# Seam halves: splitting two layer ends by tokens and moving norm factors to the products in a three-layer block on one core

## The chip, the cores and the metric

One NeuronCore of a Trainium2 chip runs the whole program. The metric is the device time of one execution in microseconds. Engines: TensorE (PE) for matmuls, VectorE (DVE) and ScalarE (ACT) for elementwise work, GpSimd (POOL), which here mostly issues a few stores, and SyncE (SP), which issues the loads.

## The reference, cut to what matters

A sequence of 256 tokens with 2048 features passes two "hybrid" layers and one block of another kind. All is float32.

```python
def hybrid_layer(x, mem, w_in, ..., w_out, ln_g, ln_b):      # twice
    h = x @ w_in                                             # 2048 x 6672
    y = concat([y_a * silu(a_z), y_b * silu(b_z), y_m * silu(m_z)])   # three kinds of attention
    return layer_norm(DEEPNORM_ALPHA * x + y @ w_out, ln_g, ln_b)

def rms_norm(x, w):
    return x * rsqrt(mean(x * x) + RMS_EPS) * w

def second_block(x, ...):
    h = rms_norm(x, norm_mix_pre)
    a_q, a_f, a_i, a_g, b_q, b_k, b_v, b_f, g_a, g_b = split(h @ w_in)   # 2048 x 11272
    y_a = hgrn2_mixer(a_q, a_f, a_i, a_g, ...) @ w_up_a
    y_b = fox_mixer(b_q, b_k, b_v, b_f) @ w_up_b
    merged = sigmoid(g_a) * y_a + sigmoid(g_b) * y_b
    x = x + rms_norm(merged @ w_o, norm_mix_post)
    h = rms_norm(x, norm_ffn_pre)
    gate, up = split(h @ w_ffn_in)                           # 2048 x 11264
    return x + rms_norm((silu(gate) * up) @ w_ffn_down, norm_ffn_post)
```

## The kernel before, in words

Every float32 product is made of three fp32r products of high and low parts (high times high, high times low, low times high). An activation matrix is held feature-major as `Split` tiles: for each of 16 feature tiles of 128, a high part and a low part of 256 tokens. `X` is the input of the layer at hand, `Y` the gated attention output that goes into `w_out`.

Weights come in *units* of 128x1024 float32 (512 KB). `plan`, `plan_f`, `plan_t` write down the order of all units once; `send` loads unit n into one of five buffers `raw` (its DMA waits until `split` has read the unit five earlier); `split` makes its high part on ScalarE (`wh<-raw`, a copy with rounding) and its low part on VectorE (`wl<-raw,wh`, a subtraction). There are four places `wh`/`wl`. `take` hands out the next unit and first splits up to two units further (`AHEAD`).

A *feature-major* group (`plan_f`, `cols_f`, `unit_f`) computes 512 output columns: two halves of four units each, 16 matmuls a unit (eight of 512 columns, eight of 256). Its result is feature-major, its two parts are added in `join` (ScalarE copies one part, VectorE adds the other). A *token-major* group (`plan_t`, `cols_t`, `token_steps`) has eight units of 12 matmuls of 512 columns, its output has tokens on partitions, and it runs for two token halves t = 0, 1 (128 tokens each) into two PSUM banks.

The order on each engine is the order in which the Python code appends operations with `op`; each engine works its list strictly in order and waits on semaphores. Elementwise work that may be late is written as generators: `posts` (stepped once a unit by `step_all`) and two `lanes` (attention pieces, stepped by `step_lane`); `finish_posts` forces the rest out at once. Attention lanes put matmuls of their own into TensorE's order.

Two places are called **seams** here: the end of layer 1 (the second hybrid layer, `l_ == 1`) before the second block, and the end of the second block's mixer before the FFN. At each a norm over all 2048 features must be known, the rows are turned by TensorE transposes (four 128x128 into one bank) and split into `X` anew before the next group can start. The seam's last token-major group runs with `late=True`: its last four units are all taken, then run for token half 0, then for half 1 (5.4 us each), so that half 0's norm work lies beside half 1's matmuls. Then `normalize_gained` (or `post_norm`) does half 1: row statistics, factor, two operations a half of the columns, sum of squares; `to_features` turns `z_buf` (or `x_buf2`), multiplies each 128x256 piece by gain and by a row `f_row` of the rms factors, and splits it into `X`. The first group after the seam, `cols_f_both`, is feature-major with its two halves run together, unit by unit as the pieces of `X` come. Layer 0's end is another matter: there the memory projections of layer 1 run in between, and nothing of it is changed.

```python
def normalize_gained(t, d, rg, rb):
    ...
    for c in range(2):
        d = z = (z - mean) * g_bc          # VectorE, 128x1024, L59
        d = z = z * r + b_bc               # VectorE, 128x1024, L59
        ... squares(t, c, zt, ...)         # ScalarE, 128x1024
```

After the seam before the FFN come eleven pairs of groups (gate, up), all feature-major, into `hraw[n]`; group 0 of the products is split into `first_h`.

## Time and profile before

| | |
|---|---|
| time, median of 3 runs (lowest, highest) | 2448.6 us (2448.51, 2449.38) |
| time of the profiled execution | 2452.5 us |
| span of its profile | 2450.7 us |
| TensorE / weight loads busy | 2407.2 us (98%) / 2076.5 us (85%) |
| VectorE / ScalarE busy | 1499.5 us (61%) / 1267.3 us (52%) |
| mean granted TensorE clock | 0.993 |
| DMA, mean over the span | 187 GB/s, 458.84 MB |

The span runs from the first to the last instruction of the profiled execution; the time beside it also holds what lies around it. Positions (such as 943.46) are microseconds from the start of the span. "Busy" is the time in which an engine has an instruction in work; waits are what lies between. The granted clock is a share of 2.4 GHz.

### The profile page before, as it was taken

The page shows a single profiled execution, that of the slowest core. Times are in us where ns is not written, and L with a number is a line of the kernel's source. Part 1 is how long each engine was busy: PE and PEld are TensorE (multiplying, and loading weights), DVE is VectorE, ACT ScalarE, POOL GpSimd, SP SyncE. Part 2 cuts the span into 40 slices and gives each one's busy share as a digit, 9 for nine tenths or more (in the row PEclk, how much of TensorE's full clock was granted, in tenths as well). Part 3 has the DMA queues.
Part 4 walks back from the last instruction along what each step waited for, and adds up shares of the span by engine and source line. Part 5 has one row for each costly group of instructions (what it writes and reads, how often), then busy time and mean ns, then how long its engine had stood idle before and what let it go on. Part 6 is the DMA issues. An engine that isn't in the chain of part 4 may idle for free.

```text
span 2450.7 us, 32972 instructions
## 1 busy us (share of the span) xinstructions
PE 2407.2 (98%) x13098; PEld 2076.5 (85%) x13098; DVE 1499.5 (61%) x1693; ACT 1267.3 (52%) x1710; POOL 7.5 (0%) x14
## 2 busy tenths in 40 slices
PE   8999999999999998999999999998999999999998
PEld 7888888888888877888898888887888888888887
DVE  6575566766755667575765566755655555555454
ACT  5444465444455644555664457444554555554443
POOL 0000000000000000000000000000000000000000
PEclk9999999999999998999999999998999999999999
DMA  8544557665545664554545545575556565557554
GB/s 297 196 152 151 178 171 258 217 218 172 163 147 172 235 204 147 181 164 155 164 155 183 177 156 181 185 244 179 197 174 195 183 195 192 182 187 256 191 196 138
DMA packets 127834, 458.84 MB, mean 187 GB/s; under 512 B 13600, under 2 KB 20288, under 8 KB 124736
## 3 DMA queue, kind: packets, MB, share of 16 engines
q1 hardware_dynamic: 126720, 450.38, 55.9%
q0 software_dynamic: 816, 6.29, 0.7%
q8 instruction: 102, 1.67, 0.3%
q14 instruction: 52, 0.43, 0.1%
q10 hardware_dynamic: 144, 0.07, 0.0%
HBM read 448.30 MB, written 8.39 MB: 186 GB/s over the span
## 4 chain that ended last, share of the span: by engine, by line
PE 92%; DVE 3%; ACT 3%; DMA 1%; issue 1%; DVEq 0%; SPq 0%; ACTq 0%
PE banks L83 91%; ACT wh L47 1%; DMA raw<-in_w_in_f 1%; PE banks L86 1%; DVE wl L50 1%; ACT tb L47 0%; DVE z_buf L59 0%; ACT sm_s L47 0%; DVE le L50 0%; DVE f_buf L59 0%; DMA raw<-in_kv_t 0%; DVE lqe L50 0%; DVE x_buf L59 0%; ACT t L47 0%; DVE o_buf L50 0%
## 5 line engine op out<-in xcount | busy, mean ns | idle before, releaser
L50 DVE TENSOR_TENSOR wl<-raw,wh 128x1024 fp32r<-128x1024 f32 x808 | 974.8, 1222 | 412.1 <-ACT wh L47 406.3
L47 ACT ACTIVATE wh<-raw 128x1024 fp32r<-128x1024 f32 (+1 forms) x811 | 835.6, 1051 | 386.2 <-PE banks L83 275.8
L83 PE MATMUL banks<-xx,wh 128*128 128x512 f32 (+1 forms) x3888 | 983.7, 395 | 2.3 <-ACT xx L47 2.3
L83 PEld LDWEIGHTS banks<-xx,wh 128*128 128x128 f32 (+1 forms) x3888 | 699.4, 189 | 135.4 <-ACT xx L47 3.0
L83 PEld LDWEIGHTS banks<-xx,wl 128*128 128x128 f32 x3840 | 525.1, 191 | 38.1
L83 PE MATMUL banks<-xx,wl 128*128 128x256 f32 x3840 | 536.3, 283 | 0.0
L83 PE MATMUL banks<-wh,xx 128*128 128x512 f32 x1536 | 383.5, 390 | 0.0
L83 PEld LDWEIGHTS banks<-wh,xx 128*128 128x128 f32 x1536 | 286.9, 188 | 59.0
L83 PE MATMUL banks<-wl,xx 128*128 128x512 f32 x768 | 207.9, 389 | 0.0
L83 PEld LDWEIGHTS banks<-wl,xx 128*128 128x128 f32 x768 | 144.2, 188 | 30.0
L83 PE MATMUL banks<-wh,yy 128*128 128x512 f32 x512 | 127.7, 390 | 3.7 <-ACT wh L47 3.7
L83 PEld LDWEIGHTS banks<-wh,yy 128*128 128x128 f32 x512 | 95.6, 188 | 25.1 <-ACT wh L47 5.4
L47 ACT ACTIVATE le<-le 128x512 f32<-128x512 f32 (+1 forms) x32 | 27.1, 846 | 89.4 <-DVE le L50 82.9
L83 PE MATMUL banks<-wl,yy 128*128 128x512 f32 x256 | 69.1, 389 | 0.0
L50 DVE TENSOR_TENSOR hraw<-banks,hraw 128x512 f32<-128x512 f32 x22 | 15.2, 691 | 84.1 <-ACT hraw L47 84.1
L47 ACT ACTIVATE hraw<-banks 128x512 f32<-128x512 f32 x22 | 13.2, 598 | 100.8 <-PE banks L83 99.1
L83 PE MATMUL banks<-yy,wh 128*128 128x512 f32 x256 | 64.1, 392 | 0.0
L47 ACT ACTIVATE z<-banks 128x512 f32<-128x512 f32 x26 | 15.5, 597 | 92.8 <-PE banks L83 92.8
L50 DVE TENSOR_TENSOR z<-banks,z 128x512 f32<-128x512 f32 x26 | 18.0, 691 | 70.7 <-ACT z L47 70.7
L83 PEld LDWEIGHTS banks<-wl,yy 128*128 128x128 f32 x256 | 48.1, 188 | 10.0
L83 PEld LDWEIGHTS banks<-yy,wh 128*128 128x128 f32 x256 | 46.1, 189 | 8.2
L68 DVE COPY_PREDICATED lacc<-cst,banks 128x256 f32<-128x256 int32 (+1 forms) x64 | 36.4, 627 | 14.6 <-PE banks L83 14.6
(203 smaller groups left out, 1570.4 us busy)
## 6 DMA issues: line engine op xcount, KB each, us to landing
raw<-in_w_in_f SPq DMA_DIRECT2D x304, 512.0 KB, 3.7
raw<-in_w_ffn_f SPq DMA_DIRECT2D x176, 512.0 KB, 4.4
raw<-in_w_ffn_down SPq DMA_DIRECT2D x88, 512.0 KB, 3.5
raw<-in_w_in_t SPq DMA_DIRECT2D x80, 512.0 KB, 3.6
raw<-in_w_out_t SPq DMA_DIRECT2D x64, 512.0 KB, 4.7
raw<-in_w_o_t SPq DMA_DIRECT2D x32, 512.0 KB, 4.4
raw<-in_kv_t SPq DMA_DIRECT2D x16, 512.0 KB, 5.3
raw<-in_kv_f SPq DMA_DIRECT2D x16, 512.0 KB, 4.4
```

What stands on the lines that cost most here:

```text
L47: return lambda e: e.activation(*a, **k)
L50: return lambda e: e.tensor_tensor(*a, **k)
L68: return lambda e: e.copy_predicated(*a, **k)
L83: return lambda e: e.matmul(*a, **k)
L86: return lambda e: e.transpose(*a, **k)
```

## The change

- At both seams, token halves go through everything apart. The next group is token-major; its first four units are run for token half 0 as soon as that half is in `X`, then for half 1 (`half_pass`, `cols_t_halves`). Transposes are made for one token half and four feature tiles at a time (`turn_half`), appended by hooks within the passes. In the text (t, q) is the piece of `X` of token half t and feature tiles 4q to 4q+3.
- For layer 1 to the second block: only `(z - mean) * r` is made before the transposes (`scaled`, one tensor_scalar 128x1024); gain and bias, multiplied by the next norm's gain (`gw3`, `bw3`), are put on after them (`gained`: VectorE for even q, four ScalarE Identities for odd q). The row `z * g + b` is finished later, one 128x1024 operation a unit (`finish_sum`), for the store and the sum of squares.
- The rms factor is no more in `X`: it goes onto products (`join(..., row=...)`, one more VectorE 128x512 for each half group; `value` for token-major ones).
- `more_places` gives the last three groups before each seam four more `wh`/`wl` places, and `take` runs up to six units ahead there.
- The first group of the second block is now the token-major `HI` group; in the FFN gate and up group 0 become token-major (`gate_rows`, `product_rows`, with eight more transposes).
- The start: eleven matmuls of zeros that nobody reads, the first piece of `memT` in two, and the load of `cst` after unit 16.

The core of the diff:

```diff
+        def more_places(offsets, fence):
+
+            for k in offsets:
+                h, l = at(f"xh{len(extra)}_{k}", k, 1024, f32r), at(f"xl{len(extra)}_{k}", k + 4, 1024, f32r)
+                extra.append((h, l))
+                places.insert(0, (extra[-1], fence, fence))
+            state["ramp"] = len(offsets)
...
+        def take(ahead=None):
 
             n = state["next"]
             state["next"] += 1
-            while len(cut) < min(n + ahead + 1, len(units)):
+            if state["ramp"]:
+                state["ramp"] -= 1
+                state["ahead"] += 1
+            while len(cut) < min(n + (state["ahead"] if ahead is None else ahead) + 1, len(units)):
...
+        def half_pass(act, pr, t, ns, k0, begin, end, keep, waits=None, hooks={}):
+
+            for u, n in enumerate(ns):
+                if u in hooks:
+                    hooks[u]()
+                his, los = [], []
+                for kk in range(2):
+                    a, b = token_steps(act, banks[pr[t]], t, (k0 + 2 * u + kk) % KT, *place[n], kk,
+                                       begin and u + kk == 0, end and u == 3 and kk == 1)
+                    his += a
+                    los += b
+                tok = run_unit(n, his, los, waits[u] if waits else (), keep)
...
+        def cols_t_halves(made, first_hooks, between, second_hooks, rest):
+
+
+            pr = pair()
             ns = [take(0) for _ in range(4)]
-            toks = []
-            for t in range(2):
-                for u, n in enumerate(ns):
-                    his, los = [], []
-                    for kk in range(2):
-                        a, b = token_steps(act, banks[pr[t]], t, (nk - 8 + 2 * u + kk + first) % nk, wh[n % NH], wl[n % NH], kk,
-                                           False, u == 3 and kk == 1)
+            free = [bank_free[pr[t]] for t in range(2)]
+            half_pass(X, pr, 0, ns, 0, True, False, True, [made[0, u // 2] + (free[0] if u == 0 else ()) for u in range(4)], first_hooks)
+            state["ahead"], state["leave"] = AHEAD, True
+            between()
+            half_pass(X, pr, 1, ns, 0, True, False, False, [made[1, u // 2] + (free[1] if u == 0 else ()) for u in range(4)], second_hooks)
+            rest()
...
+                tok = run_unit(n, his, los, made[0, u // 2] + made[1, u // 2])
...
+        def keep_awake(n, tile, bank, waits=()):
+
+            waits += bank_free[bank]
+            for _ in range(n):
+                mm(lambda e: e.matmul(banks[bank][:, :], tile, tile.rearrange("p (o c) -> p o c", o=1).to_broadcast([P, 4, P]),
+                                      start=True, stop=True), *waits)
+                waits = ()
...
+            if row is not None:
+                r2 = row[0].rearrange("p (o s) -> p o s", o=1).to_broadcast([P, 2, S])
+                d = op("dve", lambda e: e.tensor_tensor(d2, d2, r2, ALU.mult), d, row[1])
...
+        keep_awake(11, asleep[:, :], 7, (op("dve", lambda e: e.memset(asleep[:, :].bitcast(f32), 0.0)),))
...
+        def scaled(t, c, waits):
+            zt = z_buf[:, t * D + c * 1024:t * D + (c + 1) * 1024]
+            return op("dve", lambda e: e.tensor_scalar(zt, zt, st[:, 64 + 2 * t:65 + 2 * t], st[:, 68 + t:69 + t],
+                                                       ALU.subtract, ALU.mult), *waits)
+
+        f_free, made, turned = [(), ()], {}, {}
+
+        def gained(t, q):
+
+            b, tok = turned[t, q]
+            f3, b3 = (x.rearrange("p (k s) -> p k s", s=P) for x in (f_buf[:, (q % 2) * 512:(q % 2) * 512 + 512], banks[b][:, :]))
+            if q % 2:
+                for j in range(4):
+                    k = 4 * q + j
+                    d = op("act", lambda e: e.activation(f3[:, j, :], b3[:, j, :], ACT.Identity, scale=gw3[:, k:k + 1], bias=bw3[:, k:k + 1]),
+                           tok, made_g, made_b, *f_free[q % 2])
+                bank_free[b] = (d,)
+            else:
+                w3, c3 = (x[:, 4 * q:4 * q + 4].rearrange("p (k o) -> p k o", o=1).to_broadcast([P, 4, P]) for x in (gw3, bw3))
+                d = op("dve", lambda e: e.tensor_tensor(f3, b3, w3, ALU.mult), tok, made_g, *f_free[q % 2])
+                bank_free[b] = (d,)
+                d = op("dve", lambda e: e.tensor_tensor(f3, f3, c3, ALU.add), d, made_b)
+            return f3, (d,)
+
+        def hi_lo(t, q, f3, tok):
+            h, l = (x[:, :, t * P:(t + 1) * P] for x in (X.hi(4 * q, 4), X.lo(4 * q, 4)))
+            c = op("act", lambda e: e.activation(h, f3, ACT.Copy), *tok)
+            d = op("dve", lambda e: e.tensor_tensor(l, f3, h.bitcast(f32), ALU.subtract), c, *tok)
+            f_free[q % 2] = (d,)
+            made[t, q] = (c, d)
+
+        def turn3(t, qs, bs, z):
+            for q, b in zip(qs, bs):
+                turned[t, q] = b, turn_half(z_buf, t, q, b, (z,))
+
+        tok0 = half_pass(Y, pr, 0, tok, 0, False, True, True)
+        ag, r = standardize(0, add(0, tok0))
+        z0 = [scaled(0, c, (ag, r)) for c in range(2)]
+        tok1 = half_pass(Y, pr, 1, tok, 0, False, True, False, hooks={2: lambda: turn3(0, (0, 1), (4, 5), z0[0])})
+        g0, g1 = gained(0, 0), gained(0, 1)
+        hi_lo(0, 0, *g0)
+        sums = add(1, tok1)
+        hi_lo(0, 1, *g1)
+        ag, r = standardize(1, sums)
+        z1 = [scaled(1, 0, (ag, r))]
+
+        def between3():
+            turn3(0, (2, 3), (4, 5), z0[1])
+            g = gained(1, 0), gained(1, 1)
+            for q in range(2):
+                hi_lo(1, q, *g[q])
+            z1.append(scaled(1, 1, (ag, r)))
+            split(len(cut))
...
+                hi_lo(0, q, *gained(0, q))
+            split(len(cut))
...
+        def rest3():
+            for q in range(2, 4):
+                hi_lo(1, q, *gained(1, q))
+            split(len(cut))
...
+                    if last:
+                        sums()
+                    d = op("dve", lambda e: e.tensor_tensor(zt, zt, g_bc[:, cc], ALU.mult), turned[t, 2 * c][1], turned[t, 2 * c + 1][1], rg)
+                    yield
...
+        def feature4(t, q, free):
+
+            b, tok = turned[t, q]
+            w = NFP(4 * q, 4).rearrange("p (k o) -> p k o", o=1).to_broadcast([P, 4, P])
+            f3 = f_buf4[:, (q % 2) * 512:(q % 2) * 512 + 512].rearrange("p (k s) -> p k s", s=P)
+            h, l = (x[:, :, t * P:(t + 1) * P] for x in (X.hi(4 * q, 4), X.lo(4 * q, 4)))
+            d = op("dve", lambda e: e.tensor_tensor(f3, banks[b][:, :].rearrange("p (k s) -> p k s", s=P), w, ALU.mult), tok, *f_free[q % 2])
+            bank_free[b] = (d,)
+            a = op("act", lambda e: e.activation(h, f3, ACT.Copy), d, *free)
+            d = op("dve", lambda e: e.tensor_tensor(l, f3, h.bitcast(f32), ALU.subtract), a, *free)
+            f_free[q % 2] = (d,)
+            made[t, q] = (a, d)
...
+        tok0 = half_pass(X, pr, 0, tok, 8, False, True, True)
+        r = last_block(0, tok0)
+        z0 = [post_sum(0, c, (r, rx) + toks[0]) for c in range(2)]
+        tok1 = half_pass(X, pr, 1, tok, 8, False, True, False, hooks={2: lambda: turn4(0, (0, 1), (4, 5), z0[0])})
+        feature4(0, 0, (tok0,))
+        r = last_block(1, tok1)
+        feature4(0, 1, (tok0,))
+        z1 = [post_sum(1, 0, (r, rx) + toks[1])]
+        factors4, squares4 = [], []
+
+        def between4():
+            turn4(0, (2, 3), (4, 5), z0[1])
+            for q in range(2):
+                feature4(1, q, (tok1,))
+            z1.append(post_sum(1, 1, (r, rx) + toks[1]))
+            split(len(cut))
...
+            for q in range(2, 4):
+                feature4(0, q, (tok0,))
+            split(len(cut))
```

## Rows read from the trace of the kernel before

**Rows 1.** The page, busy time (share of the span) and instructions of each engine.

```profile
PE 2407.2 (98%) x13098; PEld 2076.5 (85%) x13098; DVE 1499.5 (61%) x1693; ACT 1267.3 (52%) x1710; POOL 7.5 (0%) x14
```

**Rows 2.** Waits of TensorE over the span: total, times, longest, in us.

```profile
...
PE banks L86 <- DVE z_buf L59: 8.4, 1, 8.4
PE banks L86 <- DVE x_buf L59: 4.9, 1, 4.9
PE banks L83 <- DVE lqe L50: 2.5, 4, 0.8
```

**Rows 3.** Windows: stretch, length, busy PE PEld DVE ACT POOL (count), clock, DMA.

```profile
...
4.00:6.00 2.00, 0.00 (x0) 0.00 (x0) 0.00 (x0) 1.06 (x1) 0.00 (x0) 1.00 1.06 424
...
1050.00:1100.00 50.00, 49.12 (x291) 43.02 (x290) 40.04 (x60) 30.96 (x44) 0.00 (x0) 1.00 0.54 173
...
1750.00:1800.00 50.00, 50.00 (x288) 43.98 (x287) 28.42 (x29) 24.97 (x32) 0.00 (x0) 1.00 0.61 203
...
2250.00:2300.00 50.00, 50.00 (x222) 41.39 (x222) 24.90 (x21) 21.06 (x21) 0.00 (x0) 1.00 0.58 193
```

**Rows 4.** Timeline of the start: start, length, engine, operation, count.

```profile
...
6.20 1.06 ACT L47 ACTIVATE wh<-raw 128x1024 fp32r<-128x1024 f32 x1 [0.23 <-DMA raw<-in_kv_t]
...
7.37 3.75 PE L83 MATMUL banks<-wh,mem 128*128 128x512 f32 x8 [7.37 <-ACT wh L47]
...
12.38 2.01 PE L83 MATMUL banks<-wh,mem 128*128 128x512 f32 x8
```

**Rows 5.** Timeline of the seam at the end of layer 1.

```profile
...
940.14 0.20 ACT L47 ACTIVATE st<-st 128x1 f32<-128x1 f32 x1
...
942.85 0.61 PE L83 MATMUL banks<-wl,yy 128*128 128x512 f32 x2
...
959.30 3.75 PE L83 MATMUL banks<-xx,wh 128*128 128x512 f32 x8 [1.15 <-ACT xx L47]
...
964.40 0.46 PEld L86 LDWEIGHTS banks<-cst,z_buf 128*128 128x128 f32 x4
```

**Rows 6.** Windows of half a microsecond at both seams.

```profile
...
947.00:947.50 0.50, 0.00 (x0) 0.00 (x0) 0.50 (x1) 0.50 (x2) 0.00 (x0) 0.82 0.00 0
...
964.00:964.50 0.50, 0.50 (x5) 0.50 (x5) 0.50 (x1) 0.00 (x0) 0.00 (x0) 0.61 0.00 0
...
1698.00:1698.50 0.50, 0.32 (x2) 0.36 (x3) 0.11 (x2) 0.50 (x2) 0.00 (x0) 0.75 0.00 0
...
1711.50:1712.00 0.50, 0.50 (x4) 0.50 (x4) 0.25 (x1) 0.22 (x1) 0.00 (x0) 0.60 0.00 0
```

**Rows 7.** Timeline of the seam before the FFN.

```profile
...
1689.97 0.20 ACT L47 ACTIVATE st<-st 128x1 f32<-128x1 f32 x1
...
1692.70 0.61 PE L83 MATMUL banks<-wl,xx 128*128 128x512 f32 x2
...
1707.70 3.75 PE L83 MATMUL banks<-xx,wh 128*128 128x512 f32 x8 [1.15 <-ACT xx L47]
...
1712.39 0.46 PEld L86 LDWEIGHTS banks<-cst,x_buf 128*128 128x128 f32 x4
```

**Rows 8.** Groups by shape: operation, count, busy us, mean ns, idle before.

```profile
...
L50 DVE TENSOR_TENSOR wl<-raw,wh 128x1024 fp32r<-128x1024 f32 x808 | 974.8, 1222 | 412.1 <-ACT wh L47 406.3 <-PE banks L83 3.6
...
L50 DVE TENSOR_TENSOR xx<-f_buf,xx 128x512 fp32r<-128x512 f32 x16 | 10.9, 684 | 0.0
...
L59 DVE SCALAR_TENSOR_TENSOR x_buf<-o_buf,st,x_buf 128x1024 f32<-128x1024 f32 x4 | 5.0, 1280 | 1.2 <-ACT st L47 1.2
...
L53 DVE TENSOR_SCALAR tb<-tb 128x512 f32<-128x512 f32 x2 | 0.9, 426 | 0.1
...
L47 ACT ACTIVATE xx<-f_buf 128x512 fp32r<-128x512 f32 x16 | 10.1, 631 | 23.9 <-DVE f_buf L59 23.9
...
L47 ACT ACTIVATE sm_s<-sm_s,st 128x128 f32<-128x128 f32 x24 | 9.3, 397 | 0.2
...
L47 ACT ACTIVATE ident_r<-cst 128x128 fp32r<-128x128 f32 x1 | 0.3, 303 | 0.0
```

More of the change, by code:

```diff
@@ L269, in plan_narrow, with give_back @@
             plan(w, hi="narrow")
-        sent, cut = [], []
-        used = {}
+        sent, cut, t_const = [], [], []
+        place = {}
+        places = [((wh[n], wl[n]), (), ()) for n in range(NH)]
+        extra = []
+        def more_places(offsets, fence):
[4 more added lines that the diff above has]
+            state["ramp"] = len(offsets)
+        def give_back(n, hi_tok, lo_tok):
+            if not (state["leave"] and any(place[n] is x for x in extra)):
+                places.append((place[n], (hi_tok, cut[n][1]), (lo_tok,)))
         def send(n):
@@ L317, in split @@
                 later.append(low)
-        state = {"next": 0}
+        state = {"next": 0, "ahead": AHEAD, "ramp": 0, "leave": False}
         lanes = ([], [])
@@ L504, in narrow_f, with spread_row @@
+        def spread_row(row, cols, b):
+            for t in range(2):
+                col, t_col = cols[t]
+                tok = op("pe", lambda e: e.matmul(banks[b][:, t * P:(t + 1) * P], col.to_broadcast([P, P]), ident,
+                                                  start=True, stop=True), t_col, *bank_free[b])
+            d = op("dve", lambda e: e.tensor_copy(row, banks[b][:, 0:S]), tok)
+            bank_free[b] = (d,)
+            return d
         def narrow_f(act, waits=()):
@@ L517, in narrow_f, with narrow_sum @@
                 w = ()
-            used[n] = (tok, tok)
+            give_back(n, tok, tok)
             return pr[0], tok
-        def narrow_sum(b, tok, rows, dst, tmp, waits=(), bias=None):
+        def narrow_sum(b, tok, rows, dst, tmp, waits=(), bias=None, row=None):
             p = banks[b]
@@ L1378, in half @@
             def half(i, pr, tok):
-                d = join(pr, tok, gates[n][:, i * 512:(i + 1) * 512], waits=free(i))
+                d = join(pr, tok, gates[n][:, i * 512:(i + 1) * 512], waits=free(i), row=rows[0])
                 posts.append((None, gate_post(i, d, n)))
@@ L1400, in build @@
             toks = list(c_ready)
-            cols_f(X, joined(toks, q_, scale=SC, waits=free))
-            cols_f(X, joined(toks, k_, waits=free))
+            cols_f(X, joined(toks, q_, scale=SC, waits=free, row=rows[0]))
+            cols_f(X, joined(toks, k_, waits=free, row=rows[0]))
             pr, tok = cols_t(X)
-            ready = tuple(toks) + evac(pr, tok, v_, waits=free)
+            ready = tuple(toks) + tuple(value(v_[:, t * 512:t * 512 + 512], pr[t], tok, factor3[t], free) for t in range(2))
             def add_decay(o, h, t, nk, g=g):
@@ new lines, in build, with rest4 @@
+        r = last_block(1, tok1)
[8 more added lines that the diff above has]
+            split(len(cut))
+            for q in range(2, 4):
+                feature4(0, q, (tok0,))
+            split(len(cut))
+        def rest4():
+            for q in range(2, 4):
+                feature4(1, q, (tok1,))
+            split(len(cut))
@@ L1567, in gate_half @@
             z, u, tmp = z4[:, c], u2[:, c], t2[:, c]
-            d = join(pr, tok, z, waits=mult_free[i])
+            d = join(pr, tok, z, waits=mult_free[i], row=rows4)
             yield
```

479 lines of the change are left out of this document (246 added, 233 removed).

## The prediction, made before the changed kernel ran

> **What bounds the kernel now.** I read the page's busy shares first, then TensorE's waits, then windows of fixed length, and last the timeline where the waits lie. TensorE is busy 2407.2 of 2450.7 us [rows 1], so only the 43 us in which it stands, and the time at its lower clock, can be won. VectorE at 61% and ScalarE at 52% have room on average, which says nothing of a seam, where everything waits for them. There are three large places: the start (nothing before 7.37 [rows 4]), and the transposes' waits for z_buf, 8.4 us at the end of layer 1, and for x_buf, 4.9 us before the FFN [rows 2].
>
> At full clock 50 us hold 288 matmul records of feature-major groups, 16 to a unit, so 2.78 us a unit, and 222 of token-major ones, 12 to a unit, so 2.70 us [rows 3]; I use 2.79 and 2.72, half a token-major unit (one token half) 1.36, four transposes 0.45 [rows 5].
>
> **The three losses, in the trace.** Start: first matmul at 7.37, its eight take 3.75 us where eight take 2.01 at 12.38 [rows 4]. So unit 0 takes 5.0 instead of 2.7 us: 7.4 us of standing and 2.3 of low clock.
>
> Seam 1: the last pass ends at 943.46, the next unit's matmuls start at 959.30 (eight in 3.75 us again) and the transposes behind that unit at 964.40 [rows 5]. That is 21.1 us from the last issue slot (0.15 before the end). The work in it at full clock is one unit 2.79, twenty transposes 2.25 and two small matmuls 0.45, so 5.5; lost are 15.6 us. Seam 2 in the same way, 1693.31 to 1712.39 [rows 7]: 19.2 less 5.5, 13.7 us lost. Clock: it falls 3.9 us after work ended at seam 1 (0.82 in the half microsecond from 947.0) and 4.9 us after at seam 2 (0.75 from 1698.0); it is back 5.1 and 4.2 us after the first unit's start (0.61 from 964.0, 0.60 from 1711.5) [rows 6]. 1.00 is 2.4 GHz, 0.50 is 1.2.
>
> **Start, after the change.** The first piece of memT is half as long, 256 KB less ahead of the first weights. DMA moves 424 GB/s there [rows 3], so the first weight split starts 0.6 us earlier than 6.20, and TensorE at 6.75. The eleven unread matmuls take 11 x 0.44 (3.75/8 less the last one's tail) = 4.9 us; they wait only for a small DVE memset and run from about 1.5 to 6.4, which is 4.9 us of matmuls where 4.2 and 5.1 raised the clock. Unit 0 then takes 2.7. Gain 0.6 + 2.3 = 2.9, less 0.1 for the ragged end: 2.8. Bounds: 0.6 (clock not up), 3.0. The consts DMA (1.1 MB) leaves the crowded first 15 us and is not needed until the kv groups end; I cost it at nothing, under cover of raw's five buffers.
>
> **Seam 1, after the change.** PE no longer stands while all 2048 columns are summed; there are now two half passes of the next group (4 units, 8 x 1.36 = 10.9 us) and 32 transposes (3.6) to do in between. What sets the time is now when each 4-tile group of X is split. I follow the three queues in program order. Durations [rows 8]: a VectorE 128x512 operation 0.69, a weight low 1.23, a ScalarE copy of 128x512 0.63. tensor_scalar 128x1024 isn't shown; 128x512 takes 0.43, so 0.75 is twice that with a fixed 0.1 counted once (bounds 0.65 and the 1.28 of a 128x1024 scalar_tensor_tensor). Four ScalarE Identities 128x128 with column scale and bias aren't shown; the copy takes 0.30, exp with a column 0.40, so 1.3 for four (1.2 to 1.6).
>
> Token half 0: the factor is there at 940.34 as before [rows 5], z0 first half 941.04; TensorE comes to the hook at 940.76 (pass start 938.0 plus 2.72) and stands 0.4. Transposes, two VectorE operations, ScalarE (its four Identities for tile group 1 stand ahead, to 943.55), copy, low: X(0,0) at 944.9. TensorE, done with pass 1 at 944.8, stands 0.25. VectorE then does sum and statistics of half 1, low of (0,1), and the factor is at 947.85, z1's first half at 948.6; TensorE reaches that hook at 949.1, no wait. From the transposes' result (949.75) VectorE's chain runs: gain and bias 1.4, wait for ScalarE 1.0, two lows 1.4, second half's scaling 0.75, weight low 1.2, gain and bias of (0,2) 1.4, ScalarE 0.7, low 0.7, ScalarE (four Identities, copy) 1.3, low 0.7, the next weight (waits 0.4) 1.6, gain and bias of (1,2) 1.4, ScalarE 0.7, low 0.7. Sum 14.9: X(1,2) is there at 964.65. The passes meanwhile need (1,0) at 952.9 (wait 0.7) and end at 959.3. The fifth unit needs (0,2) and (1,2): it **stands 5.4 us**, 959.3 to 964.8. I count 0.57 + 0.25 + 0.71 + 5.45 = 7.0 us of waits where 15.6 were lost: gain **8.6** at full clock.
>
> **Seam 2, after the change.** The same walk from 1690.17, when the factor is there [rows 7], with a 128x1024 scalar_tensor_tensor (1.28, 1.24 when queued) for each sum and, on each tile group, one VectorE operation, a copy and a low. Here every group goes VectorE, ScalarE, VectorE with nothing between, and (0,1) stands behind ScalarE's square and the reduction of half 1. TensorE waits 1.1 at the first hook (z0 at 1691.4), 1.4 for (0,1) (1699.1), 0.3 at the last hook, and 5.5 for (1,2): from the transposes' result at 1701.25 there are five rounds of 0.69 + 0.63 + 0.69 with two hand-overs, 2.09 each, for (1,0), (1,1), (0,2), (0,3) and (1,2), the sum's 1.24, two weight lows of 1.23 and 0.4 of waiting for the second one's high part: 14.5, so 1715.8. The passes end at 1710.4. Sum 8.3, gain **5.4**.
>
> **The clock.** Both new waits, 5.4 and 5.5 us, are longer than the 3.9 and 4.9 us after which the clock had fallen [rows 6]. The fifth unit then starts at 1.2 GHz and stays there some 4.2 to 5.1 us, half of it lost: **2.3** a seam, 4.6. The Trainium skill (TensorE: Matmul & The Clock Gate, HAM oscillation) says the same in general, that a wait in the middle of a kernel brings the low clock back and its climb is paid again; by this case's rows it holds here, and without it the time would be 4.6 us less.
>
> **The rest.** Two FFN groups become token-major, 16 x 0.07 = 1.1 won; eight more transposes for their product 0.9 lost. +0.2. The factors on products are one more VectorE 128x512 (0.69) behind each join, some 36 in the second block and 40 in the FFN, 52 us; each lies beside 2.79 us of TensorE, and VectorE has 10 us in 50 free even in the fullest stretch [rows 3]. Deferred sums: eight of 1.28, one a unit, 1.28 + 1.23 < 2.79, hidden; without the cover they would cost 10 us. Behind them the forget posts now end just before the linear attention starts. Its matmuls stand in TensorE's order, and waited 2.5 us in four [rows 2]. I add 1.0 for that (0 to 3.5). The extra weight places: four more splits in 11 us make VectorE late by about 2 us, and two units ahead (5.4 us) cover it; nothing.
>
> On the four Identities the Trainium skill (VectorE: DVE Perf Modes, the TRN2 errata) has a cycle table by which a ScalarE read of 128 from PSUM is 0.25 us, 1.0 for four. By the page the sum would win another 0.9 us; no row here shows the operation.
>
> **Sum.** 2.8 + 8.6 + 5.4 - 4.6 + 0.2 - 1.0 = 11.4. The profiled execution took 2452.5 us (span 2450.7 and 1.8 around it), so 2441.1; the median of the runs is 3.9 lower, 2448.6, so **2437.2**. My own range for this case: 2434 to 2440.
>
> **Rivals.**
> - *The waits are short enough for the clock* (0.20). If VectorE and ScalarE overlap better, the fifth unit waits under 3.9 us and the clock stays: 4.6 and some 3 of waiting come back, 2430; with one seam, 2434. For it: queued operations follow a little closer than their own durations. Against: the chain is dependent, a round trip at each group.
> - *The waits are longer* (0.15). If the scaling takes 1.28 and each hand-over 0.1 more, each fifth unit waits 8 us: 5 less won, and with the start's clock not raised another 2.2; 2442 to 2444, up to no measurable change.
> - *VectorE becomes the bound beside the linear attention* (0.05). It is busy 40.0 of 50 us from 1050 [rows 3]. If each of the some 22 visits of the two groups' attention to TensorE comes one row product (0.69) later with nothing to hide it, 15 us: 2452, slower. It decides from 17 visits on.
> - *The change doesn't do what it says at the start*: unread matmuls too late or too few; 2439.4. It lies within the first case's neighbourhood and is counted there (about 1 in 8 of it).
> - The likeliest: 0.60.
>
> **Range and chances.** A measurement of this kernel tells 0.2% (4.9 us) from nothing, so faster is below 2443.7: 0.60 + 0.20, and 0.06 of the long waits' 0.15; the other 0.09 and 0.01 of the attention's case lie within 0.2%, 0.04 above it. The range takes in the short waits and the better part of the long ones: 2430 to 2443.
>
> **What would show it.** Right: first eight real matmuls in about 2.0 us at 6.8; two waits of TensorE for ACT or DVE xx of 5 to 6 us, about 15.8 us after each token half's second pass; granted clock 0.50 for some 4 to 5 us right behind them, and not earlier; hooks' waits under 1.5; waits for lqe about as before. Wrong: no clock drop (short waits), a wait behind the deferred sums, ScalarE's Identities at 0.4 each, or new waits for wh as the extra places fill.

## The result and the profile after

The changed kernel takes 2454.07 us (median of 15 runs, 2451.81 to 2455.65), beside 2448.93 us for the kernel before on the same chip (15 runs, 2446.33 to 2449.93). The ratio is 1.0021, 95% interval 1.0014 to 1.0028: 5.1 us slower where 11.4 us faster was forecast. The profiled execution took 2454.99 us, 0.9 above its median; the one of before lay 3.9 above its own. So the traces explain only 2.5 us between the two kernels. The rest is where each profiled execution lies among its kernel's runs.

The page of the changed kernel: busy time of each engine, and the granted clock in 40 slices of the span.

```profile
...
PE 2411.8 (98%) x13053; PEld 2076.3 (85%) x13053; DVE 1543.8 (63%) x1756; ACT 1278.9 (52%) x1730; POOL 7.5 (0%) x14
...
PEclk9999999999999999989999999999999999999999
```

Against [rows 1], VectorE and ScalarE are still far from full on average. The new thing is the eighteenth slice of the clock row, 1042 to 1104 us, which is an 8. Next, the waits of TensorE over the whole span.

```profile
PE banks L83 <- DVE xx L50: 11.6, 5, 4.8
PE banks L83 <- DVE lqe L50: 8.5, 5, 3.5
PE banks L83 <- ACT wh L47: 5.0, 5, 1.5
PE banks L86 <- DVE crow L62: 2.7, 1, 2.7
...
PE banks L86 <- DVE x_buf L59: 1.0, 1, 1.0
PE banks L86 <- DVE z_buf L53: 0.6, 1, 0.6
```

The waits for z_buf and x_buf of [rows 2] have shrunk from 13.3 to 1.6 us, and two waits of 4.8 us for pieces of X stand in their place: the two fifth units, as forecast. But the waits for lqe, 2.5 us in four before, are 8.5 us in five. That row is the one that the prediction called "about as before".

**Where the time went.** Each line is the start of the same TensorE instruction in both traces, so the last column says how far the changed kernel is ahead (negative) or behind at that point.

| place | before | after | after less before |
|---|---|---|---|
| first use of mk and q (layer 1's attention) | 130.0 | 128.7 | -1.3 |
| second token half's pass, seam 1 | 937.9 | 933.9 | -4.0 |
| first products of negative and ident_r (second attention) | 1346.0 | 1352.4 | +6.4 |
| last transposes of sm_s before seam 2 | 1466.5 | 1473.5 | +7.0 |
| first use of first_h (FFN, second matrix) | 2202.7 | 2205.2 | +2.5 |
| end of the span | 2450.7 | 2453.2 | +2.5 |

By the work between 934 and 968 us, counted as in the prediction, the waits and low clock of seam 1 come to 9.0 us where 15.6 were lost: 6.6 won, so the kernel is 10.6 ahead at 968 us. By 1352 us it is 6.4 behind. **Seventeen microseconds are lost in 380**, most of them beside the linear attention's first group. A wait for sm_s that is 0.6 us longer (1.28 for 0.64) follows, and seam 2 then wins 4.5 back (7.0 to 2.5 behind).

The first 2.7 us of this table (from 1.3 to 4.0 ahead, between 130 and 934 us) are luck. From the first use of mk to the first sum into z_buf the traced execution of before takes 808.1 us. The kernels of experiments 3 and 4, which are the kernel before in that stretch, take 805.0 and 804.8, and the nine traced executions with the change 804.7 to 806.2. So the execution of before that stands in the table was some 3 us slow there, which is most of the 3.9 by which it lies above its median.

**The start.** The timeline of TensorE: start, length, count, and in brackets how long it stood and for whom.

```profile
1.05 5.06 PE L83 MATMUL banks<-asleep 128*128 128x512 f32 x11 [1.05 <-DVE asleep L80]
...
7.36 2.12 PE L83 MATMUL banks<-wh,mem 128*128 128x512 f32 x8 [1.24 <-ACT wh L47]
...
10.95 2.11 PE L83 MATMUL banks<-wh,mem 128*128 128x512 f32 x8 [0.56 <-ACT wh L47]
```

The unread matmuls do raise the clock: eight real ones take 2.12 us where [rows 4] had 3.75. But the first of them starts at 7.36, not 6.75, and the second unit stands 0.56 us more. The first weights' split starts at 6.25 us, no earlier than in [rows 4]. That is this one execution: of the ten traced executions with this start, eight begin that split at 5.08 to 5.37 us and two at 6.25 and 6.68. The two traced ones with the old start have 6.20 and 6.31.

**Seam 1.** TensorE, and the VectorE and ScalarE work that X(0,2) and X(1,2) wait for (timeline, same columns).

```profile
...
946.66 1.51 ACT L47 ACTIVATE f_buf<-banks,cst 128x128 f32<-128x128 f32 x4 [2.66 <-PE banks L86]
...
949.56 1.15 PE L83 MATMUL banks<-wh,xx 128*128 128x512 f32 x4 [0.69 <-DVE xx L50]
949.93 0.81 DVE L53 TENSOR_SCALAR z_buf<-z_buf,st 128x1024 f32<-128x1024 f32 x1
950.65 1.22 DVE L50 TENSOR_TENSOR xl<-raw,xh 128x1024 fp32r<-128x1024 f32 x1
...
955.55 0.61 PE L83 MATMUL banks<-xl,xx 128*128 128x512 f32 x2
...
956.90 1.23 DVE L50 TENSOR_TENSOR xl<-raw,xh 128x1024 fp32r<-128x1024 f32 x1 [0.25 <-ACT xh L47]
958.04 0.68 DVE L50 TENSOR_TENSOR f_buf<-banks,cst 128x512 f32<-128x512 f32 x1
...
960.99 3.75 PE L83 MATMUL banks<-xh,xx 128*128 128x512 f32 x8 [4.82 <-DVE xx L50]
```

This is the forecast chain, instruction for instruction: two small waits, the fifth unit standing 4.82 us (5.4 forecast), and its eight matmuls at half speed. The two lows of weights (xl<-raw,xh, 1.22 and 1.23 us) lie inside the chain. They are the fifth and the sixth unit's own.

**Beside the linear attention.** All three engines from the join of k, in the second group's forget scans, to the wait for lqe.

```profile
1043.92 0.69 DVE L50 TENSOR_TENSOR k<-banks,k 128x512 f32<-128x512 f32 x1 [1.81 <-ACT k L47]
...
1044.65 0.69 DVE L50 TENSOR_TENSOR k<-k,cst 128x512 f32<-128x512 f32 x1
...
1045.37 0.64 ACT L47 ACTIVATE t<-k 128x512 f32<-128x512 f32 x1 [1.48 <-DVE k L50]
...
1046.58 1.04 ACT L47 ACTIVATE wh<-raw 128x1024 fp32r<-128x1024 f32 x1
...
1047.65 1.23 DVE L50 TENSOR_TENSOR wl<-raw,wh 128x1024 fp32r<-128x1024 f32 x1 [2.31 <-ACT wh L47]
1048.85 0.69 DVE L50 TENSOR_TENSOR u<-u,t 128x512 f32<-128x512 f32 x1
1049.58 0.69 DVE L50 TENSOR_TENSOR t<-u,k 128x512 f32<-128x512 f32 x1
1050.19 0.69 DVE L50 TENSOR_TENSOR lqe<-k,le 128x512 f32<-128x512 f32 x1
1050.79 0.68 DVE L50 TENSOR_TENSOR lqe<-q,le 128x512 f32<-128x512 f32 x1
...
1051.57 3.65 PE L83 MATMUL banks<-lqe 128*128 128x64 f32 x16 [3.49 <-DVE lqe L50]
...
1054.98 3.18 PE L83 MATMUL banks<-xx,wh 128*128 128x512 f32 x8
```

The same place in the kernel before:

```profile
1050.63 1.05 ACT L47 ACTIVATE wh<-raw 128x1024 fp32r<-128x1024 f32 x1
1050.77 0.69 DVE L50 TENSOR_TENSOR k<-banks,k 128x512 f32<-128x512 f32 x1 [1.67 <-ACT k L47]
...
1051.69 0.64 ACT L47 ACTIVATE t<-k 128x512 f32<-128x512 f32 x1
...
1052.86 0.69 DVE L50 TENSOR_TENSOR lqe<-k,le 128x512 f32<-128x512 f32 x1
...
1055.19 0.69 DVE L50 TENSOR_TENSOR u<-u,t 128x512 f32<-128x512 f32 x1
```

There, lqe starts 2.1 us after the start of the join of k, behind one low of a weight. In the changed kernel it starts 6.3 us after it. Three things make up the 4.2 us. The row product takes 0.7. The two sums of the forget post, u and t, now stand ahead of lqe: 1.4. And the low of the weight waits 2.31 us for ScalarE's high part, where it waited 0.26: another 2.1. On ScalarE the post's first stage (t<-k and t<-t, its Abs and Exp) now stands ahead of the copy wh<-raw, and must itself wait for k. So half of VectorE's delay is a wait, not work.

The row product apart, the instructions are the same ones; the reason is in forget_half. Its join is now the first stage of the post, and the post is stepped once at the half's end. So every stage is issued one unit earlier than before: the first one ahead of the next weight split, the second one ahead of the lane's visit. The next post does the same to the next lqe, 2.78 us at 1070.27. The first group's second forget half has this order too, and there TensorE itself stands 1.52 us for wh at 1015.14.

Windows of the granted clock, at seam 1, at this wait and at the next, and then the 50 us that [rows 3] has at full clock (columns: stretch, length, busy PE, PEld, DVE, ACT, POOL with counts, clock, DMA share, GB/s).

```profile
958.00:958.50 0.50, 0.00 (x0) 0.00 (x0) 0.50 (x2) 0.00 (x0) 0.00 (x0) 0.86 0.00 0
...
1050.50:1051.00 0.50, 0.00 (x0) 0.00 (x0) 0.50 (x2) 0.50 (x2) 0.00 (x0) 0.52 1.03 401
...
1071.00:1077.00 6.00, 6.00 (x22) 5.23 (x21) 5.01 (x9) 2.51 (x5) 0.00 (x0) 0.50 0.63 204
...
1050.00:1100.00 50.00, 45.39 (x235) 40.06 (x235) 34.78 (x55) 24.93 (x32) 0.00 (x0) 0.86 0.40 134
```

The clock fell 2.4 us after TensorE had run dry at 1048.1, and stayed at 1.2 GHz to 1057.4. The window from 1050 to 1100 us holds 235 matmuls where [rows 3] has 291.

### The profile page after: what moved, and what is told of

Same layout as the page of the kernel before. It is cut to its first block, busy times and chain, and to the rows that moved or that the text cites. A ratio compares the mean times of both kernels' runs of the same rounds, so it can differ in the third digit from the quotient of the medians.

```text
span 2453.2 us, 32936 instructions
## 1 busy us (share of the span) xinstructions
PE 2411.8 (98%) x13053; PEld 2076.3 (85%) x13053; DVE 1543.8 (63%) x1756; ACT 1278.9 (52%) x1730; POOL 7.5 (0%) x14
## 4 chain that ended last, share of the span: by engine, by line
PE 91%; DVE 4%; ACT 3%; issue 1%; DMA 1%; SPq 0%; DVEq 0%; ACTq 0%
PE banks L83 90%; ACT wh L47 1%; DVE wl L50 1%; PE banks L86 1%; DMA raw<-in_w_in_f 0%; ACT tb L47 0%; ACT t L47 0%; DMA raw<-in_kv_t 0%; ACT xx L47 0%; DVE f_buf L50 0%; DVE x_buf L59 0%; DVE k L50 0%; ACT sm_s L47 0%; DVE lqe L50 0%; DVE xx L50 0%
## 5 line engine op out<-in xcount | busy, mean ns | idle before, releaser
L50 DVE TENSOR_TENSOR wl<-raw,wh 128x1024 fp32r<-128x1024 f32 x776 | 936.6, 1221 | 398.3 <-ACT wh L47 396.5
L47 ACT ACTIVATE wh<-raw 128x1024 fp32r<-128x1024 f32 (+1 forms) x779 | 803.3, 1051 | 353.2 <-PE banks L83 245.2
L83 PE MATMUL banks<-xx,wh 128*128 128x512 f32 (+1 forms) x3760 | 951.3, 395 | 1.5 <-ACT wh L47 1.5
L83 PEld LDWEIGHTS banks<-xx,wh 128*128 128x128 f32 (+1 forms) x3760 | 676.6, 189 | 130.2 <-ACT wh L47 1.7
L83 PEld LDWEIGHTS banks<-xx,wl 128*128 128x128 f32 x3712 | 507.0, 190 | 36.8
L83 PE MATMUL banks<-xx,wl 128*128 128x256 f32 x3712 | 517.9, 282 | 0.0
L83 PE MATMUL banks<-wh,yy 128*128 128x512 f32 x416 | 103.5, 390 | 1.6 <-ACT wh L47 1.6
L83 PE MATMUL banks<-xh,xx 128*128 128x512 f32 x160 | 44.6, 418 | 10.7 <-DVE xx L50 10.7
L50 DVE TENSOR_TENSOR xl<-raw,xh 128x1024 fp32r<-128x1024 f32 x32 | 38.6, 1223 | 19.3 <-ACT xh L47 19.0
L47 ACT ACTIVATE xh<-raw 128x1024 fp32r<-128x1024 f32 x32 | 33.2, 1056 | 30.2 <-PE banks L83 16.8
```

The costliest lines, as they stand in the source:

```text
L47: return lambda e: e.activation(*a, **k)
L50: return lambda e: e.tensor_tensor(*a, **k)
L83: return lambda e: e.matmul(*a, **k)
```

## The experiments

Ten runs of nine kernels. Each ratio is to the kernel before on the same chip, whose median was 2448.61, 2448.84 and 2448.76 us in the three sets. Differences to the changed kernel (2454.07 us, ratio 1.0021, from a set of its own) are taken from the medians.

**1. The forget posts in the old order.** Only the second group's: the join is issued at once again, and every stage of the post a unit later. The row product stays.

```diff
             def forget_half(i, pr, tok, g=g, k_=k_, b_=b_, forget=forget):
+                if g == 1:
+                    d = join(pr, tok, k_[:, i * 512:i * 512 + 512], row=rows[0])
+                    posts.append((None, forget_post(i, d, g, k_, b_, forget)))
+                    return
                 posts.append((pr, forget_join(i, pr, tok, g, k_, b_, forget)))
```

> The changed kernel, with one thing undone: in the second group (g = 1) of the second block the join of a forget half and its row product are appended at once and the post begins one step later, as before the change. Theory A (order): the change lets the post's first stage start at the half's end, so its second stage (ScalarE Ln and Relu, two VectorE additions) comes into the queues ahead of the lane's two lqe products of the same step, and TensorE, which stands at the lane's matmuls, waits for the whole chain. Then the two long waits for lqe (3.5 and 2.8 us) shrink to about 1 us and less, the clock's two falls from 1050 to 1078 are gone (3 us each), and the time falls by 9 to 11 us, from 2454 to about 2444. Theory B (the row product itself is what is late): the products are still there, so the waits stay near 3 us and the time within 2 us of 2454.

2443.53 us, ratio 0.9978 (0.9969 to 0.9987): 10.5 us less than the changed kernel. VectorE and TensorE at the same place:

```profile
1044.43 0.69 DVE L50 TENSOR_TENSOR lqe<-k,le 128x512 f32<-128x512 f32 x1
...
1045.03 0.68 DVE L50 TENSOR_TENSOR lqe<-q,le 128x512 f32<-128x512 f32 x1
...
1045.96 1.90 PE L83 MATMUL banks<-lqe 128*128 128x64 f32 x16
1046.89 0.69 DVE L50 TENSOR_TENSOR u<-u,t 128x512 f32<-128x512 f32 x1
```

TensorE does not stand at all there, the sixteen matmuls take 1.90 us in place of 3.65, and the clock is 1.00 from 1040 to 1100 us. The low of the weight (1043.30) starts right behind the row product, so its wait for ScalarE is gone too. Two thirds of the 16 us that the stretch lost beyond forecast are this one thing. How its 10.5 us divide between the earlier first stage (on ScalarE) and the earlier sums (on VectorE) no run tells; by the rows above the two are 2.1 and 1.4 us of VectorE's delay.

**2. The row product left out.** The second group's forget halves are joined without the multiplication by the factor row, so that its k and forget gates lack the norm's factor.

```diff
-                d = join(pr, tok, k_[:, i * 512:i * 512 + 512], row=rows[0])
+                d = join(pr, tok, k_[:, i * 512:i * 512 + 512], row=rows[0] if g == 0 else None)
```

> The changed kernel without the row product (VectorE 128x512, 0.69 us) on the two forget halves of g = 1; this part of the norm is left out. Theory A (order): the chain stays ahead of lqe, each long wait shrinks by at most 0.7 us (3.5 to 2.8, 2.8 to 2.1), and the time falls by 1.5 us, or by up to 5 if a shorter wait spares one fall of the clock. Theory B (row product): both waits go back to 0.7 us and below, as in the kernel before, and the time falls by about 10 us.

2450.81 us, ratio 1.0009 (1.0000 to 1.0018): 3.3 us less, with an interval that still overlaps the changed kernel's (1.0014 to 1.0028). The waits for lqe between 1010 and 1120 us are 5.9 us, where the changed kernel has 7.4, and the clock still falls (0.68 from 1050 to 1060 us). Two operations of 0.69 us, 1.4 together, in a queue that is already late cost 3.3: 1.5 in the waits for lqe, the rest not placed. They make the waits longer; they don't make them: VectorE still stands 2.31 us for wh ahead of the low, and TensorE 2.72 us for lqe.

**3. The kernel before, with the new posts.** The converse: nothing of the change but the stepping of the second group's forget posts.

```diff
+                if g == 1:
+                    def joined_post():
+                        d = join(pr, tok, k_[:, i * 512:i * 512 + 512])
+                        yield from forget_post(i, d, g, k_, b_, forget)
+                    posts.append((pr, joined_post()))
+                    step_posts()
+                    return
```

> The kernel before, with one thing of the change put in: the join of each forget half of the second group is the first stage of its post, and that post is stepped once at the half's end, so that its stages come one unit earlier among the linear attention's. Theory A (that order alone puts the two sums and a weight split ahead of lqe): TensorE waits of 2.5 to 3.5 us for lqe between 1050 and 1110 us, the clock falling after two of them, and 5 to 10 us slower than before, 2454 to 2459 us. Rival B (it needs the change's row products or its earlier phase as well): within 2 us of before's 2448.6, waits for lqe under 1 us.

2458.06 us, ratio 1.0040 (1.0028 to 1.0053): 9.2 us **slower** than before. So the order alone brings the loss; it needs neither the row product nor the rest of the change. VectorE's low waits 2.31 us for wh here as well (at 1050.63).

```profile
1051.83 0.69 DVE L50 TENSOR_TENSOR u<-u,t 128x512 f32<-128x512 f32 x1
1052.56 0.69 DVE L50 TENSOR_TENSOR t<-u,k 128x512 f32<-128x512 f32 x1
1053.16 0.68 DVE L50 TENSOR_TENSOR lqe<-k,le 128x512 f32<-128x512 f32 x1
...
1054.55 3.65 PE L83 MATMUL banks<-lqe 128*128 128x64 f32 x16 [4.27 <-DVE lqe L50]
```

**4. The start alone,** on the kernel before: the unread matmuls, memT in smaller first pieces, and the constants' transfer sent 16 transfers later.

```diff
+        asleep = at("asleep", 100, P, f32r)
+        keep_awake(11, asleep[:, :], 7, (op("dve", lambda e: e.memset(asleep[:, :].bitcast(f32), 0.0)),))
...
-        plan_t(A["kv_t"][0, 0], among=pieces("memT", M))
+        plan_t(A["kv_t"][0, 0], among=pieces("memT", M, ((0, 2), (2, 2), (4, 4), (8, 4), (12, 4))), early=True)
```

> The kernel before with the change's start alone: eleven unread matmuls, memT's first piece in two, cst after unit 16. By the traces the changed kernel is 1.3 us ahead at the first memory attention, so 2448.9 becomes about 2447.6. My prediction had 2.8 us, 2446.1. If the late load of cst costs something later, no gain at all.

2447.20 us, ratio 0.9992 (0.9983 to 1.0001): 1.4 us less than before. The interval, 4.2 us less to 0.2 more, takes in no change, the 1.3 us that the changed kernel leads at 128.7 us, and the 2.8 forecast; it can't tell them apart. The traces say a little more. The ten traced executions with this start reach the first use of mk at 127.1 to 129.9 us, on average 128.3, and the two with the old start at 130.0 both: 1.7 us on average.

**5. The seams with the weights' splits behind the pieces of X.** No part of the computation changes. Two things move, at both seams: the splits of weights are issued behind the pieces of X, and the first step of the piece (0,3) (at seam 1 its four Identities) is issued ahead of the low of (0,2).

```diff
-            split(len(cut))
+            g = gained(0, 2), gained(0, 3)
             for q in range(2, 4):
-                hi_lo(0, q, *gained(0, q))
-            split(len(cut))
+                hi_lo(0, q, *g[q - 2])
...
                 hi_lo(1, q, *gained(1, q))
+                split(len(cut))
             split(len(cut))
```

> The changed kernel with another order in both seams, the work being the same: the two weight splits that stood between X(1,1) and X(1,2) come behind the pieces of X that the fifth unit needs, and the ScalarE or VectorE first step of (0,3) is begun before the low part of (0,2). Theory A (the fifth unit waits for X(1,2), and that for a chain of hand-overs between VectorE and ScalarE with two weight lows in it): its wait of 4.8 us falls to about 1.6 at each seam, the clock does not fall there, and each seam is 3.2 + 2.0 us shorter, 10 us together, 2444. Rival (total VectorE work sets it, whatever its order): the wait moves to the sixth or seventh unit and the time changes by less than 3 us.

2442.98 us, ratio 0.9979 (0.9970 to 0.9987): 11.1 us less than the changed kernel. The waits of TensorE from 925 to 975 us:

```profile
PE banks L83 <- ACT xh L47: 0.9, 1, 0.9
PE banks L83 <- DVE xx L50: 0.9, 2, 0.7
PE banks L86 <- DVE z_buf L53: 0.6, 1, 0.6
```

and the window on the same stretch, which the changed kernel passed with 198 matmuls at a clock of 0.93:

```profile
925.00:975.00 50.00, 47.69 (x230) 38.73 (x229) 34.71 (x42) 24.85 (x46) 0.00 (x0) 1.00 0.39 123
```

The 4.8 us were not the price of the seam. At seam 1, X(1,2) is there 4.7 us after the passes' end in the changed kernel and 0.6 us after it here. Of these 4.1 us, about 2.7 are the two lows of weights with the wait for their high part, and 1.4 is VectorE's wait for the Identities of (0,3), which is gone. The weights are not free, though: they are the fifth and sixth units' own, and now the fifth stands 0.88 us for its high part (xh), 0.94 at seam 2. With the wait that short the clock stays up too. No run moves the splits alone.

**6. The clock's share by itself.** The changed kernel, with 18 unread matmuls in each fifth unit's wait; X itself comes as late as it did.

```diff
             rest()
+            keep_awake(18, X.hi_of(0, 0, P), 2 if pr[0] == 0 else 0)
             for u in range(4, 8):
```

> The changed kernel with 18 unread matmuls of 128x512 ahead of the fifth unit of each seam, where it waits 4.8 us for its pieces of X; the wait itself stays. Theory A (the fall of the clock costs 2.0 to 2.3 us a seam beside the wait): the clock at full through both seams, the fifth unit's eight matmuls in 2.0 in place of 3.75 us, and 4.0 to 4.6 us less than the changed kernel, 2449.5 to 2450.1 us. Rival B (what TensorE gains there is taken up by the next wait for weights or by lqe): within 1.5 us of the changed kernel's 2454.1.

2448.40 us, ratio 0.9999 (0.9991 to 1.0008): 5.7 us less than the changed kernel.

```profile
954.67 4.24 PE L83 MATMUL banks<-xx 128*128 128x512 f32 x18
959.65 2.09 PE L83 MATMUL banks<-xh,xx 128*128 128x512 f32 x8 [0.74 <-DVE xx L50]
```

The eight matmuls take 2.09 in place of 3.75 us at either seam. The whole fifth unit takes 2.84 us in place of 4.78 at seam 1 and 4.71 at seam 2, so the clock cost 1.9 us a seam, 3.8 together (4.6 forecast). The trace has another 1.0 in shorter waits for lqe (6.4 for 7.4 us between 1010 and 1120 us); the last 0.9 is not placed.

**7. Both edits together** (1 and 5), run in two sets.

> The changed kernel with both earlier edits together: the posts of the second group's forget scans one stage later, as in the kernel before, and at the two seams the splits of the weights behind the pieces of X that a unit waits for. Theory A (the two losses are separate places of time, 10.5 and 11.1 us as each gave alone): the gains add, 2454.1 - 21.6 = 2432.5 us (2430 to 2436), TensorE waits under 1 us at the fifth units, the clock full at both seams and at full from 1040 to 1100 us. Rival B (both edits gain by shifting the lane's phase, so that the second finds nothing left between 1000 and 1350 us): 2441 to 2444 us.

> The kernel with both edits again, on the same chip as the one with the unread matmuls at crow, to compare the two: 0.9939 of before, as in its first runs (0.993 to 0.995).

2433.72 and 2433.52 us, both 0.9939 of before (0.9927 to 0.9952 and 0.9925 to 0.9952). That is 20.4 us less than the changed kernel and 15.1 and 15.2 less than before; the two gains alone add to 21.6. They are separate places of time.

**8. The next wait, for crow.** The kernel of 7 with one more yield ahead of crow's transposes, so that another unit comes before them.

```diff
                     yield
+                    yield
                     n_ = op("dve", lambda e: e.tensor_scalar(neg, crow[:, :], -1.0, None, ALU.mult), d)
```

> The last kernel with one more yield before the transposes of crow, so that TensorE has another unit of the gate's columns ahead of them. Theory A (the wait of 2.7 us for crow and the fall of the clock after it are loss): the wait goes, the clock stays at full from 1015 to 1040 us, 3 to 5 us less than the last kernel, about 2428.5 us. Rival B (the same VectorE queue only makes the next instruction wait, lqe in place of crow, for about as long): within 1.5 us of the last kernel.

2432.20 us, ratio 0.9931 (0.9918 to 0.9945): 1.5 us less than the kernel of 7 in the same set, with intervals that overlap. In the profiled executions its span is 0.7 longer (2431.7 for 2431.0). The rival is right: the wait for crow is gone and the next instruction has it.

```profile
1030.51 0.65 DVE L50 TENSOR_TENSOR lke<-k,le 128x512 f32<-128x512 f32 x1
1031.09 0.67 DVE L50 TENSOR_TENSOR lqe<-q,le 128x512 f32<-128x512 f32 x1
...
1031.91 1.43 PE L83 MATMUL banks<-lqe,lke 128*128 128x128 f32 x8 [4.01 <-DVE lqe L50]
```

VectorE makes lke and lqe right behind crow. Whichever of them TensorE asks for first, it stands for the same queue, and the clock falls either way (0.83 from 1030 to 1040 us).

**9. Unread matmuls at crow.** The kernel of 7, with nine ahead of the two transposes.

```diff
+                    keep_awake(9, X.hi_of(0, 0, P), 4)
                     w = (d,) + bank_free[4]
```

> The kernel with both edits (posts of the second group later, splits at the seams behind the pieces of X), and nine unread matmuls of 128x512 ahead of the two transposes of crow, where TensorE waits 2.7 us. Theory A (the fall of the clock to half at that wait is a cost beside the wait): no slice under full clock from 1030 to 1040 us, the eight matmuls of lqe and lke and the unit behind them at full speed, and 1.5 to 2.3 us less than the kernel with both edits: ratio to before about 0.9931 in place of 0.9939. Rival B (the time comes back as a longer wait for lqe, which VectorE makes about 1 us after crow): the wait for lqe grows from 0.8 to about 1.2 us or more, and under 0.7 us is left of the gain.

2432.64 us, ratio 0.9937 (0.9925 to 0.9949), 0.9 less than the kernel of 7 in the same set and not told apart from it. The clock is kept: 1.00 from 1030 to 1040 us. The eight matmuls of lqe and lke take 1.13 us, where they took 1.73, and the next eight 2.09 for 3.19: 1.7 us of work at low clock saved. But the time is given back, as the second theory had it (waits from 1010 to 1120 us):

```profile
PE banks L83 <- DVE lqe L50: 3.1, 4, 1.1
PE banks L83 <- ACT wh L47: 1.5, 1, 1.5
PE banks L86 <- DVE crow L62: 0.7, 1, 0.7
```

The kernel of 7 waits 1.9 us for lqe there, so 1.2 are given back at once. The wait for wh is no new one: the kernel of 7 has it too, 1.52 us before 1008.86, just outside the window. From the first sum into z_buf at seam 1 to the first products of negative and ident_r, at 1335 us, both take 401.3 us. The same trick that paid 5.7 us at the seams pays nothing that can be told here. At a seam TensorE comes out of the wait with the weights of its next units split; in the lane it only arrives earlier at things that VectorE and ScalarE have still to make.

## Why the prediction was wrong

The forecast for the profiled execution was 2441.1 us, and it took 2455.0: 13.9 us off. The conversion to the median gives another 3.0, since it took off 3.9 us, and this execution lies only 0.9 above its median.

- **The start: +2.8 forecast, 1.4 by the medians (-0.2 to 4.2), 1.7 on average by the traces.** The clock came up as forecast (2.12 for 3.75 us on the first eight), but in six of ten traced executions the second unit stands for its weights (0.56 to 1.16 us), a wait that the forecast did not have. The earlier landing was not there in the profiled execution (6.25 us for 6.20), but in eight of ten it was, and by more than the 0.6 forecast (5.08 to 5.37 us). Why two of them were late is open.
- **Seam 1: +8.6 - 2.3 = 6.3 forecast, 6.6 measured.** Waits 0.57, 0.17, 0.69 and 4.82 us, where the forecast had 0.57, 0.25, 0.71 and 5.45. The operations that no row showed: tensor_scalar of 128x1024 takes 0.77 to 0.81 us (0.75 taken), and the four Identities 1.51 (1.3 taken, 1.6 the bound). On these, the cycle table of the Trainium skill (VectorE: DVE Perf Modes, the TRN2 errata) gives an estimate of 0.25 us apiece; the trace gives 0.38, and the measurement decides. The sum is right, but its view was short: it priced two weight lows and the Identities' turn as part of the chain and did not ask whether they had to stand there. Experiment 5 shows that they had not.
- **Seam 2: +5.4 + 0.2 - 2.3 = 3.3 forecast, 4.5 measured,** with waits of 0.96, 1.05, none and 4.82 us, where the forecast had 1.1, 1.4, 0.3 and 5.5.
- **The clock, 2.3 a seam: right in kind, 1.9 measured.** The two rows behind it showed that a wait in mid-kernel brings the low clock and a climb, and experiment 6 has the price without the wait. The Trainium skill (TensorE: Matmul & The Clock Gate, HAM oscillation) states it too, that a wait in the middle of a kernel brings the low clock back, and the trace agrees at both seams. But the prediction took from [rows 6] that waits under 3.9 us leave the clock up, and that was wrong: it also fell at three waits of 2.7 to 3.5 us (crow and two for lqe), which the sum did not contain.
- **Before the seam:** 2.7 us are won between 130 and 934 us that no term had. They are the luck of one execution, as the section on the result shows, and no gain of the change. TensorE waits 2.7 us for wh from 840 to 930 us in the traced execution of before; in the two other kernels that are the same in that stretch it waits 0.9 and 0.3.
- **"I add 1.0 for that (0 to 3.5)": the step that failed.** It stands under "The rest", on the forget posts and the linear attention: 17.0 us were lost there. The prediction said that the posts "now end just before the linear attention starts". That is the first group's; the **second** group's forget halves, through the same new forget_half, are computed while the first group's attention runs as a lane. There the step_posts() at a half's end is a change of order in two queues: on ScalarE the post's Abs and Exp ahead of a weight's high part, for which VectorE's low then waits 2.31 us, and on VectorE two sums ahead of lqe. By the runs: 10.5 us are that order (experiment 1; 9.2 when it is put alone into the kernel before, experiment 3), 3.3 us the row product in the same queue (experiment 2, partly the same microseconds), and the rest the wait for crow (2.7 for 1.0 us in the kernel before), one for wh of 1.5, and the clock at crow. Experiment 8 moved the wait for crow without a gain that can be told; its cause and that of the wait for wh no run tests. Of the 17.0 us, 8.9 are longer waits from 1010 to 1120 us (7.4 for lqe, 2.7 for crow and 1.5 for wh, where before has 1.7, 1.0 and none). Most of the rest, 7.6 us by the durations at either clock, is TensorE working at half clock behind three of them.

Of the rivals, the one that lay nearest by its number, "VectorE becomes the bound beside the linear attention" (2452 us), was right about the place and wrong about the mechanism. It wanted 17 of 22 visits late by one row product each. In fact there were three waits of 2.7 to 3.5 us, crow's among them, VectorE was never full (34.8 us of 50 in the worst stretch, less than the 40.0 before), and leaving out two of its row products gave 3.3 us. The question to ask was not how full VectorE is, but what stands in its queue between a lane's input and the instruction that TensorE wants.

The chance of 0.04 for slower rested on that averaging argument and on nothing that read the posts in program order. For the seams the prediction had read them so, and it got within 0.3 and 1.2 us.

## What to carry to other kernels

Where work is issued from several generators into one queue, moving a `step` by one unit costs nothing in busy time and can cost 10 us: for each moved stage, write the queue's order out at **every** place where the function is called, not at the one that the change is about. Look at each queue that feeds the awaited instruction, also at the one behind it: here half of what VectorE lost it stood for ScalarE. When a chain ends in a wait of TensorE, look first for operations in it that can stand behind it (here weight splits, and a hand-over taken in another order: 11 us together), and only then fill the wait with unread matmuls. Those pay where the work behind the wait is ready (5.7 us at the seams), and are given back where it is made just in time (0.9 us at crow).

## What was not expected of the hardware

- The granted clock fell 2.2 us after TensorE ran dry at 956.2 us, 2.4 us after at 1048.1 and 2.0 us after at 1717.5 (0.53 in the half microsecond from 1719.5). Behind the waits for crow and for the second lqe it fell 3.8 and 3.5 us after TensorE ran dry, the latter when TensorE was at work again. In the kernel before it took 3.9 and 4.9 us at the seams [rows 6]. A wait of 2.06 us for lqe brought a fall in experiment 2 (at 1069.9 us) and none in experiment 3 (behind 1073.81). Ahead of 956.2, TensorE had stood three times (0.57, 0.17 and 0.69 us) and made thirty-two small transposes within 20 us. Ahead of 1048.1 it had been busy for 11 us without a break, the first 3.2 of them at low clock. No run here tells what makes the difference.
- Sixteen 128x64 matmuls behind such a wait took 3.65 us at low clock; at full clock they took 1.97 us behind a wait and 1.90 without one. Eight of 128x128 took 2.05 and 1.13.
- Eighteen unread matmuls of 128x512 in 4.24 us, with 0.74 us of standing behind them, kept the clock at 1.00 through both seams; nine in 2.23 us, with 0.67 behind them, kept it at crow.
- With a first piece half as large, the first weights' split began at 5.08 to 5.37 us in eight traced executions and at 6.25 and 6.68 in two; with the whole piece it began at 6.20 and 6.31. One execution of each, as in [rows 4] and the changed kernel (6.20 and 6.25), would have hidden this.
